# Output projection by token block, and forty first keys of the expert table through dense tiles

## The chip, the cores and the metric

The kernel runs on one core of a Trainium2 chip. The core has five engines that work side by side and wait for one another through semaphores: TensorE (PE in the rows, matrix products into the eight banks of PSUM), VectorE (DVE), ScalarE (ACT), GpSimd (POOL, here used to issue gathers) and SyncE (SP, here used to issue plain transfers). Transfers from HBM run on 16 DMA engines that all queues share. The metric is the device time of one execution in microseconds, lower is better.

## What is computed

One streaming-encoder block over 256 tokens of width 2048, all in float32: a hybrid mixer (stick-breaking attention and HGRN2 recurrence, merged with gates, then `w_out`), a residual with a layer norm, a PEER feed-forward, and another residual with a layer norm. The part that matters here starts at `w_out`:

```python
y = merged @ w_out                                        # 256 x 2048 by 2048 x 2048
x = layer_norm(ALPHA * x + (1 + gate1) * y, ln1_g, ln1_b)
h = x * (1 + scale2) + shift2
q = (h @ w_q).reshape(256, 8, 2, 128)                     # 8 heads, two half keys
s_top, i_top = top_k(einsum('thpd,hpnd->thpn', q, sub_keys), 16)
best, pos = top_k(all 16 x 16 sums of the two halves, 16)
expert_idx = 128 * first_key + second_key                 # 16 experts a head and token
w = softmax(best) * gelu(einsum('td,thkd->thk', h, u_tab[expert_idx]))
y = einsum('thk,thkd->td', w, v_tab[expert_idx])          # tables of 16384 x 2048
x = layer_norm(ALPHA * x + (1 + gate2) * y, ln2_g, ln2_b)
```

## The kernel before

The 256 tokens are two blocks of 128. Up to about 843 us the kernel computes the modulation, the mixer and the gates, which the change leaves alone but for the order of the elements in `merged_t`.

**Output projection.** `w_out` is eight column chunks of 2 MB, streamed by SP through the four slots of `ring` (in `arena`). TensorE multiplies each by both blocks (`project_rows`, L884, 32 products recorded as 64), and between chunks it spreads the modulation rows over the partitions (`spread_mod_rows`, L1039). VectorE adds each chunk to the residual `xr` (L1430, L1433) and, after the last, normalises both blocks. The scale and shift columns for h come from rows that are stored to DRAM (`mod2`) and loaded back.

**First head.** TensorE turns the normed x (`turn`, L1063), makes the query of head 0 (L1079) and its key scores, and VectorE chooses the first 16 experts (`choice`, four pieces). Then POOL gathers. The queries of heads 1 to 7 (`ring`, L1195) follow on TensorE beside that.

**Rows.** There are 16 steps n (block and head) of 16 rows e. A row is one expert of each of 128 tokens. POOL gathers row (n, e) of `expert_u` and row (n-1, e) of `expert_v` (`gather_row`, L535) into two rings of five buffers each. VectorE reduces a u row against h (`reduce_row`, L1561) and ScalarE applies gelu per head. VectorE spreads the 16 weights (`weigh`, L1572). TensorE multiplies the v row into four PSUM banks (`weigh_row`, L1119, 4 products recorded as 8). POOL issues in program order, so a u row that isn't wanted yet holds back the v row behind it. The pieces of the other choices are placed among the rows by `choice_steps`, and a head's u rows wait for its choice (`s_ex`).

**Dense tiles.** Experts whose first key is at or above FIRST_DENSE = 96 are not gathered: `bounds_check` skips those indices. Each of the DENSE = 32 first keys is one tile of 128 experts instead, loaded whole (1 MB) and multiplied by all 256 tokens: first u (`dense_u_piece`, L1141, four pieces a tile, placed by `DENSE_U_AT`), then v (`dense_v_piece`, L1153, placed by `DENSE_V_AT`). 20 of the 32 u tiles stand ahead of step (5, 0) and 12 behind it.

**Mask stage.** In steps n = 5 to 8 the gates of all 256 tokens are spread over the dense tiles: four tokens a row, one product of a column mask and a row mask each (`spread_gates`, L1179). The masks are made by ScalarE and VectorE, with eight column masks in flight, and every BATCH = 16 tokens VectorE multiplies what is in PSUM into the tiles' activations (`weigh_dense`) or, for a tile that comes later, `mix` does. From n = 9 on there are only rows and v tiles, which below is called the v stage. A tail of some 35 us adds, norms and stores.

## Time and profile before

| | us |
|---|---|
| median of 3 runs | 2225.26 |
| lowest, highest | 2222.92, 2225.37 |
| the profiled execution | 2222.43 |
| its span, first to last instruction | 2220.7 |
| mean granted TensorE clock | 0.931 of full speed |
| HBM read over the span | 858.38 MB |

The times of single steps come from the one profiled execution. The profile groups them by engine and line; busy time of TensorE overlaps for neighbouring products, so stretches are read from start to start.

### The profile page before, as it was taken

To read this page: it belongs to the slowest core of one execution; us is meant where nothing else is said; L and a number is where in the kernel's file an instruction comes from. 1 tells how busy PE (TensorE), PEld (TensorE's weight loads), DVE (VectorE), ACT (ScalarE), POOL (GpSimd) and SP (SyncE) were. 2 spreads that over 40 slices of the span, in tenths; PEclk is the share of its full clock that TensorE was granted. 3 is DMA by queue.
4 is the path that set the end of the run, shared out by engine and by line. 5 is a ranking of instruction groups with operands and counts; after the bars stand their busy time and mean duration, and the time that the engine had idled before them with its cause. 6 is when DMAs were issued, how large, how long until landed. Compare 5 with 4: busy or idle time off the path is not lost.

```text
span 2220.7 us, 27840 instructions
## 1 busy us (share of the span) xinstructions
PE 1924.0 (87%) x10667; PEld 1310.0 (59%) x10667; DVE 1353.3 (61%) x2003; ACT 385.3 (17%) x1010; POOL 796.8 (36%) x556
## 2 busy tenths in 40 slices
PE   4899999999999999989788788988975778778776
PEld 4788788888888888878555455555640112112221
DVE  7832377886544541157698898767865544454547
ACT  0122222211000000022132212644430000000001
POOL 1000000000000000014565545776877765656653
PEclk9999999999999999999899999888985888998987
DMA  9973456675765746429899999999999999999997
GB/s 386 423 309 114 155 232 256 264 302 221 284 255 228 278 179 256 160 70 357 329 392 416 409 412 411 405 401 403 386 405 379 405 416 414 402 406 414 400 393 284
DMA packets 104462, 722.47 MB, mean 325 GB/s; under 512 B 29949, under 2 KB 29981, under 8 KB 32045
## 3 DMA queue, kind: packets, MB, share of 16 engines
q0 software_dynamic: 78832, 465.61, 52.7%
q1 hardware_dynamic: 25522, 255.45, 28.8%
q8 instruction: 65, 1.06, 0.2%
q14 instruction: 43, 0.35, 0.0%
HBM read 858.38 MB, written 4.21 MB: 388 GB/s over the span
## 4 chain that ended last, share of the span: by engine, by line
PE 48%; DMA 31%; DVE 8%; issue 7%; POOL 3%; ACT 1%; SPq 0%; POOLq 0%; DVEq 0%
PE ps L876 24%; DMA arena<-expert_v,expert_q 14%; DMA arena<-expert_u,expert 12%; PE ps L884 10%; PE ps L900 4%; PE ps L1119 3%; POOL arena L535 3%; DMA mod_rows<-expert_v,expert_q 2%; DVE work L1561 2%; DMA mod_rows<-expert_u,expert 2%; PE ps L1153 2%; PE ps L1141 1%; PE ps L990 1%; DMA arena<-ada_early 1%; DVE buf_a L1561 1%
## 5 line engine op out<-in xcount | busy, mean ns | idle before, releaser
L1561 DVE CUSTOM_DVE_ANT_0 work<-arena,buf_b 128x2048 f32<-128x2048 f32 x166 | 380.9, 2294 | 266.9 <-DMA arena<-expert_u,expert 266.5
L876 PE MATMUL ps<-buf_a,arena 128*128 128x256 f32 x1920 | 418.5, 379 | 0.9 <-ACT arena L618 0.9
L1119 PE MATMUL ps<-arena,mod_rows 128*32 128x512 f32 x1648 | 254.1, 697 | 188.3 <-DMA arena<-expert_v,expert_q 153.0
L535 POOL DMA_INDIRECT arena<-expert_v,expert_q x206 | 351.7, 1707 | 171.0 <-PE ps L1119 106.9
L876 PEld LDWEIGHTS ps<-buf_a,arena 128*128 128x128 f32 x1920 | 363.5, 190 | 49.9 <-issue 1.2
L535 POOL DMA_INDIRECT arena<-expert_u,expert x205 | 274.7, 1340 | 180.0 <-DVE work L1561 84.4
L523 POOL DMA_DIRECT2D arena<-ada_late x32 | 16.9, 529 | 744.6 <-DVE mod_rows L1313 614.3
L1141 PE MATMUL ps<-arena 128*128 128x256 f32 x1024 | 267.9, 413 | 5.5 <-DMA arena<-dense_u 5.5
L1141 PEld LDWEIGHTS ps<-arena 128*128 128x128 f32 x1024 | 200.0, 203 | 122.2 <-issue 88.6
L1119 PEld LDWEIGHTS ps<-arena,mod_rows 128*32 128x32 f32 x1648 | 38.3, 115 | 300.5 <-DMA arena<-expert_v,expert_q 223.3
L716 ACT ACTIVATE work<-work 32x4 f32<-32x4 f32 (+3 forms) x320 | 66.4, 207 | 556.5 <-DVE work L1561 549.1
L1313 DVE SCALAR_TENSOR_TENSOR mod_rows<-arena,cols,mod_rows 128x4096 f32<-128x4096 f32 x32 | 143.4, 4481 | 13.5 <-DMA arena<-ada_late 10.4
L1153 PE MATMUL ps<-arena 128*32 128x512 f32 x1024 | 133.8, 657 | 0.0
L1561 DVE CUSTOM_DVE_ANT_0 work<-mod_rows,buf_b 128x2048 f32<-128x2048 f32 x42 | 96.4, 2294 | 57.9 <-DMA mod_rows<-expert_u,expert 57.8
L1153 PE MATMUL ps<-arena,buf_a 128*32 128x512 f32 x1024 | 131.2, 646 | 0.0
L884 PE MATMUL ps<-arena,buf_a 128*128 128x256 f32 x512 | 112.3, 379 | 0.0
L876 PE MATMUL ps<-arena 128*128 128x256 f32 x512 | 111.8, 379 | 0.0
L884 PE MATMUL ps<-arena,buf_b 128*128 128x256 f32 x512 | 111.7, 379 | 0.0
L884 PEld LDWEIGHTS ps<-arena,buf_b 128*128 128x128 f32 x512 | 97.1, 190 | 15.7 <-issue 2.8
L900 PE MATMUL ps<-buf_a,arena 128*128 128x256 f32 x384 | 94.7, 411 | 12.3 <-ACT buf_a L591 12.3
L876 PEld LDWEIGHTS ps<-arena 128*128 128x128 f32 x512 | 97.3, 190 | 13.2
L884 PEld LDWEIGHTS ps<-arena,buf_a 128*128 128x128 f32 x512 | 96.9, 190 | 13.0
(256 smaller groups left out, 2078.7 us busy)
## 6 DMA issues: line engine op xcount, KB each, us to landing
arena<-weights SPq DMA_DIRECT2D x62, 2048.0 KB, 8.5
arena<-ada_late POOLq DMA_DIRECT2D x32, 2048.0 KB, 10.4
arena<-ada_early SPq DMA_DIRECT2D x16, 2048.0 KB, 16.9
arena<-dense_u SPq DMA_DIRECT2D x32, 1024.0 KB
arena<-expert_v SPq DMA_DIRECT2D x32, 1024.0 KB
arena<-w_early SPq DMA_DIRECT2D x8, 1536.0 KB, 8.6
arena<-expert_v,expert_q POOLq DMA_INDIRECT x206, 18.3
arena<-expert_u,expert POOLq DMA_INDIRECT x205, 18.3
```

Of the source, the lines that this page charges most:

```text
L523: pool.dma_start(ada_slot[s], ada_late[ds((i * 2 + s) * P, P), g * ADA_COLS:(g + 1) * ADA_COLS])\
L535: pool.indirect_dma_start(slot, None, table, bass.IndirectOffsetOnAxis(ap=indices[:, n // HEADS, column:column + 1], axis=0), bounds_check ...
L716: last = run(target(k, g), source(k, g), function)
L876: last = mm(ps[:, bank, c * TOKENS:(c + 1) * TOKENS], ring[slot][:, first + k, c * P:(c + 1) * P], rhs[:, k, :], start=(k == 0), stop=(k = ...
L884: last = mm(ps[:, bank, b * COLS:(b + 1) * COLS], lhs[:, k, b * P:(b + 1) * P], ring[slot][:, k, :], start=(k == 0), stop=(k == KT - 1))
L900: last = mm(ps[:, c // 2, c % 2 * TOKENS:(c % 2 + 1) * TOKENS], early_slot[g % 2][:, k, c * P:(c + 1) * P], h_t[:, 2 * g + k, :], start=fi ...
L990: last = mm(ps[:, bank + n // 4, n % 4 * P:(n % 4 + 1) * P], decay[:, n, m], decay[:, n, m], start=True, stop=True)
L1119: last = mm(ps[j * GROUP:(j + 1) * GROUP, n // HEADS * QUADS + g, :], spread_w[n % 2][:, e, :], slot[:, j * QCOLS:(j + 1) * QCOLS], start= ...
L1141: last = mm(ps[:, 4 + a % 2, 0:TOKENS], tile[:, k, :], h2_t[:, k, :], start=k == 0, stop=k == KT - 1)
L1153: last = mm(ps[j * GROUP:(j + 1) * GROUP, r, :], dense_act[a // 16][:, a % 16, r * GROUP:(r + 1) * GROUP], dense_slot[t % 2][:, j * QCOLS: ...
L1313: v.scalar_tensor_tensor(out=sums, in0=ada_slot[s], scalar=cond[:, ds(k, 1)], in1=sums, op0=ALU.mult, op1=ALU.add).then_inc(ada_used[s], 1)
L1561: v.tensor_tensor_reduce(out=products[n], in0=u_slot[s], in1=h2[:, n // HEADS], scale=1.0, scalar=0.0, op0=ALU.mult, op1=ALU.add, accum_ou ...
```

## The change

1. The output projection goes by token block (`out_product`, 16 products recorded as 32): all eight chunks for block 0 (`FIRST_OUT`), then the norm of block 0, its turn, the query and the key scores of head 0, and only then the eight chunks for block 1 (`SECOND_OUT`), with the query rows of head 1 of block 0 among them. Chunks 4 and 5 go to the former `ada_slot`s, and chunks 2, 0 and 1 are loaded a second time. VectorE adds the chunks of block 1 between the first 16 u rows (`out_steps`), and the norm of block 1 stands after row (0, 15).
2. U rows use three of their five buffers in the first eight rows (`U_ORDER`), since the others still hold chunks.
3. The scale and shift columns come from 32 one-column products (`mod2_cols`); eight of the twelve spreads and the trip through `mod2` are gone. The residual is stored without the gain and bias of the first norm, and VectorE applies these to the reloaded quarter rows at n = 12 (`residual_gain`, four operations).
4. Choices are made in the order of heads 0, 1 (block 0), 0, 1 (block 1), then 2 to 7 of each (`CHOICE_ORDER`). That of head 2 stands at rows (1, 12) to (1, 15).
5. DENSE is 40, FIRST_DENSE 88. 16 u tiles stand ahead of (5, 0), at (2, 13) to (4, 15), and 24 behind it. BATCH is 8. V tiles start at (9, 4). Reduced rows are written in place.

The core of the diff:

```diff
-DENSE = 32
+DENSE = 40
-BATCH = 512 // DENSE
+BATCH = 8
+FIRST_OUT = ((0, 0, 1), (1, 1, 1), (2, 2, 1), (3, 3, 1), (4, 4, 1), (5, 5, 1), (6, 1, 2), (7, 2, 2))
+SECOND_OUT = ((4, 4, 1), (5, 5, 1), (6, 1, 2), (7, 2, 2), (3, 3, 1), (2, 5, 2), (0, 2, 3), (1, 3, 2))
+UNITS = ((0, 0), (1, 0), (0, 1), (1, 1))
...
+        U_ORDER = [(0, 1, U_RING - 1)[row % 3] if row < TOPK // 2 else (row - 1) % U_RING for row in range(BLOCKS * HEADS * TOPK + TOPK)]
...
-        choice_steps = row_order[4:12:2] + [row_order[TOPK + i * 64 // 56] for i in range(56)]
-        dense_steps = [row_order[TOPK + FIRST_BESIDE + 1:5 * TOPK], row_order[5 * TOPK:9 * TOPK - 4]]
+        CHOICE_ORDER = [0, 1, HEADS, HEADS + 1] + list(range(2, HEADS)) + list(range(HEADS + 2, BLOCKS * HEADS))
+        choice_steps = row_order[12:16] + row_order[TOPK + 4:TOPK + 60]
+        out_steps = {(0, 0): 9, (0, 2): 10, (0, 4): 11, (0, 7): 12, (0, 11): 13, (0, 14): 14, (0, 15): 15}
+        dense_steps = [row_order[2 * TOPK + SECOND_BESIDE + 1:5 * TOPK], row_order[5 * TOPK:9 * TOPK - 4]]
-        v_steps = row_order[10 * TOPK - 3:16 * TOPK - 3]
+        v_steps = row_order[9 * TOPK + QUADS:16 * TOPK - 3]
-        BEFORE_MASKS = 20
+        BEFORE_MASKS = 16
-        ACT_DELAY, MIX_DELAY = 2, 6
+        ACT_DELAY, MIX_DELAY, STEPS_OF_BATCH = 2, 3, 2
...
+            def out_product(j):
+
+                b, (c, s, fill) = j // GATES, (FIRST_OUT + SECOND_OUT)[j]
+                if s >= 4:
+                    pe.wait_ge(late_out_loaded[s - 4], fill * 16)
+                else:
+                    pe.wait_ge(loaded[s], (F_OUT[s] + fill) * 16)
+                if j > 3:
+                    pe.wait_ge(s_y, j - 2)
+                if GATES <= j < GATES + TURNED:
+                    pe.wait_ge(s_h2, j - GATES + 1)
+                for k in range(KT):
+                    last = mm(ps[:, j % 4, 0:COLS], merged_t[:, b, k, :], ring[s][:, k, :], start=k == 0, stop=k == KT - 1)
+                last.then_inc(s_om, 1)
...
+            for j in range(GATES):
+                out_product(j)
+            spread_gate2()
+            mod2_cols(range(KT, 2 * KT)).then_inc(s_mcol, 1)
...
             turn(0, range(TURNED))
-            pe.wait_ge(loaded[0], (F_QUERY[0] + 1) * 16)
-            pe.wait_ge(s_row, 1 + 13)
-            query_of_first(0)
-            turn(1, (0, 1))
+            pe.wait_ge(s_row, 1 + 5)
+            query_rows(0)
+            turn_back(0, (0, 1))
             turn_query(0)
-            turn(1, (2, 3))
+            turn_back(0, (2, 3))
             pe.wait_ge(s_sk, 16)
...
+            score_first(0)
+            for j in range(GATES, GATES + 5):
+                out_product(j)
+            query_rows(1)
             turn_query(1)
...
+            out_product(GATES + 5)
+            score_first(1)
+            out_product(GATES + 6)
+            out_product(GATES + 7)
```

On TensorE, from the spread of the modulation rows to the first query. L1039 is a spread, L884 a chunk with both blocks, L1063 a turn, L1079 the query of head 0. Before:

```order
L1039 MATMUL ps<-mod_rows,cst 128x512 x4
L884 MATMUL ps<-arena,buf_b 128x256 x32
L1039 MATMUL ps<-mod_rows,cst 128x512 x3
L884 MATMUL ps<-arena,buf_b 128x256 x32
L1039 MATMUL ps<-mod_rows,cst 128x512 x2
...
L884 MATMUL ps<-arena,buf_b 128x256 x96
L1063 MATMUL ps<-cst,buf_a 128x128 x16
L1079 MATMUL ps<-arena 128x256 x16
L1063 MATMUL ps<-cst,buf_a 128x128 x8
```

The same place after (L1094 is a spread, L1105 the one-column products, L1120 `out_product`, L1099 the spread of gate2, L1138 a turn, L1157 query rows, L1145 a turn back, L1165 and L1175 the turn and scores of a query):

```order
L1094 MATMUL ps<-mod_rows,cst 128x512 x4
L1105 MATMUL ps<-cols,mod_rows 128x1 x16
L1120 MATMUL ps<-arena,buf_b 128x256 x128
L1099 MATMUL ps<-mod_rows,cst 32x512 x4
L1105 MATMUL ps<-cols,mod_rows 128x1 x16
L1138 MATMUL ps<-cst,buf_a 128x128 x16
L1157 MATMUL ps<-arena 128x256 x16
...
L1175 MATMUL ps<-work 128x128 x2
L1120 MATMUL ps<-arena,buf_b 128x256 x80
L1157 MATMUL ps<-arena 128x256 x16
```

Before the first turn stand 128 products of the projection instead of 256; 80 of the rest stand behind the scores of head 0, in one piece.

On TensorE in the mask stage, before (L1119 the v row, L1141 pieces of a u tile, L1179 the tokens' gates):

```order
L1119 MATMUL ps<-mod_rows 32x512 x4
L1179 MATMUL ps<-mod_rows 128x32 x4
L1119 MATMUL ps<-arena,mod_rows 32x512 x4
L1141 MATMUL ps<-arena 128x256 x4
L1179 MATMUL ps<-mod_rows 128x32 x4
L1119 MATMUL ps<-arena,mod_rows 32x512 x4
L1141 MATMUL ps<-arena 128x256 x4
L1179 MATMUL ps<-mod_rows 128x32 x4
```

After (L1210, L1242 and L1280 are the same three):

```order
L1210 MATMUL ps<-mod_rows 32x512 x4
L1242 MATMUL ps<-arena 128x256 x4
L1280 MATMUL ps<-mod_rows 128x40 x4
L1210 MATMUL ps<-arena,mod_rows 32x512 x4
L1242 MATMUL ps<-arena 128x256 x8
L1280 MATMUL ps<-mod_rows 128x40 x4
L1210 MATMUL ps<-arena,mod_rows 32x512 x4
L1242 MATMUL ps<-arena 128x256 x4
```

Every row now has one or two pieces of a tile (96 in 60 rows), where it had none or one (48).

On VectorE, in the first 16 rows after the change (L1645 is a reduced row, L1529 and L1531 add a chunk of block 1, L1536 its statistics):

```order
L1620 CAST expert<-work 128x16
L1529 SCALAR_TENSOR_TENSOR work<-mod_rows,ps 128x256
L1531 SCALAR_TENSOR_TENSOR buf_a<-buf_a,work 128x256
L1645 ISA arena,work<-arena,buf_b 128x2048
L1645 ISA work 128x1
L1529 SCALAR_TENSOR_TENSOR work<-mod_rows,ps 128x256
L1531 SCALAR_TENSOR_TENSOR buf_a<-buf_a,work 128x256
L1536 BN_STATS small<-buf_a 128x6
L1645 ISA arena,work<-arena,buf_b 128x2048
```

Before, nothing of the projection was left at this place.

## Rows read from the trace of the kernel before

**Rows 1.** The page: busy time by engine, and its 40 slices of the span.
```profile
PE 1924.0 (87%) x10667; PEld 1310.0 (59%) x10667; DVE 1353.3 (61%) x2003; ACT 385.3 (17%) x1010; POOL 796.8 (36%) x556
...
PE   4899999999999999989788788988975778778776
...
DMA  9973456675765746429899999999999999999997
```

**Rows 2.** Windows of the three stages: start:end and length, busy us, granted clock, DMA share, GB/s.
```profile
1388.70:1672.00 283.30, 240.12 (x1414) 159.75 (x1414) 205.82 (x335) 133.79 (x387) 209.33 (x129) 0.88 1.00 400
...
995.70:1388.70 393.00, 332.52 (x1669) 225.29 (x1667) 328.55 (x778) 90.86 (x261) 218.85 (x154) 0.96 0.97 389
1672.00:2190.00 518.00, 390.20 (x2992) 96.07 (x2992) 268.87 (x251) 24.22 (x113) 337.67 (x227) 0.85 1.00 400
```

**Rows 3.** Timeline of TensorE, output projection to first query: start, us, operation, records, idle before.
```profile
847.02 13.98 PE L884 MATMUL ps<-arena,buf_b 128*128 128x256 f32 x64
...
924.51 41.71 PE L884 MATMUL ps<-arena,buf_b 128*128 128x256 f32 x192
971.44 3.68 PE L1063 MATMUL ps<-cst,buf_a 128*128 128x128 f32 x16 [5.23 <-DVE buf_a L1452]
```

**Rows 4.** One-column products: duration min/median/max of the line before that has them.
```profile
L893 PEld LDWEIGHTS ps<-cols,work x64: 186/192/337, 24.2 to 126.6; 128*128 128x128 f32 x64
```

**Rows 5.** Timeline of POOL: the first gather.
```profile
995.65 2.17 POOL L535 DMA_INDIRECT arena<-expert_u,expert  x1 [12.95 <-DVE expert L1534]
```

**Rows 6.** Timeline of VectorE: first u row, last of head 0, first of head 1.
```profile
1004.14 2.29 DVE L1561 CUSTOM_DVE_ANT_0 buf_b<-arena,buf_b 128x2048 f32<-128x2048 f32 x1 [4.94 <-DMA arena<-expert_u,expert]
...
1056.57 2.29 DVE L1561 CUSTOM_DVE_ANT_0 buf_b<-arena,buf_b 128x2048 f32<-128x2048 f32 x1
...
1073.30 2.29 DVE L1561 CUSTOM_DVE_ANT_0 buf_a<-arena,buf_b 128x2048 f32<-128x2048 f32 x1 [14.44 <-DMA arena<-expert_u,expert]
```

**Rows 7.** The page: the software queue's bytes, and a gather's us from issue to landing.
```profile
q0 software_dynamic: 78832, 465.61, 52.7%
...
arena<-expert_u,expert POOLq DMA_INDIRECT x205, 18.3
```

**Rows 8.** Timeline of TensorE in the mask stage: two rows of the loop, back to back.
```profile
1406.09 1.07 PE L1119 MATMUL ps<-arena,mod_rows 128*32 128x512 f32 x8
1407.09 1.99 PE L1141 MATMUL ps<-arena 128*128 128x256 f32 x8
1408.92 0.97 PE L1179 MATMUL ps<-mod_rows 128*128 128x32 f32 x8
1409.82 1.06 PE L1119 MATMUL ps<-arena,mod_rows 128*32 128x512 f32 x8
```

**Rows 9.** Waits of TensorE in 1388:1672: in total, times, longest.
```profile
PE ps L1119 <- DMA arena<-expert_v,expert_q: 33.0, 17, 8.5
PE ps L1119 <- DVE mod_rows L1572: 5.2, 2, 3.3
PE ps L1165 <- DVE mod_rows L1572: 2.5, 1, 2.5
```

**Rows 10.** Timeline of TensorE after a long wait, at the end of the mask stage.
```profile
1660.00 1.93 PE L1119 MATMUL ps<-arena,mod_rows 128*32 128x512 f32 x8 [8.46 <-DMA arena<-expert_v,expert_q]
```

**Rows 11.** L1141 alone, in the mask stage: busy us of its products and weight loads.
```profile
1388.70:1672.00 283.30, 110.29 (x384) 78.62 (x384) 0.88 1.00 400
```

**Rows 12.** Timeline of TensorE in the v stage: a quarter of a v tile.
```profile
1750.09 1.89 PE L1153 MATMUL ps<-arena 128*32 128x512 f32 x16
```

More of the change, by code:

```diff
@@ new lines, in first_keep, with query_head @@
+            def first_keep(u, signal):
+                act_e.wait_ge(s_ks0, u + 1)
+                keep(*UNITS[u], slice(0, 2)).then_inc(signal, 1)
+            def query_head(h):
+                s = h % 2
+                act_e.wait_ge(used[s], 1 + F_QUERY[s] + h // 2 + 1)
+                run(pq_t[s], ps[:, 6 + s, :], ACT.Copy).then_inc(s_pq, 1)
+                act_e.wait_ge(s_ks, h - 1)
+                for b in range(BLOCKS):
+                    last = keep(h, b, slice(0, 2))
+                last.then_inc(s_kept, 1)
@@ L1122, in weigh_row @@
                 last.then_inc(slot_used, 1)
+            pe.wait_ge(s_wgt, 1)
+            pe.wait_ge(s_h2, TURNED + 1)
+            for e in range(2):
+                weigh_row(0, e)
+            query_rows(3)
+            turn_query(3)
+            for e in range(2, QUADS):
+                weigh_row(0, e)
+            score_first(3)
             def turn_stats(turn, groups):
@@ L1188, in score_half @@
                 return last
[L1190 removed]
+            for h in range(2, HEADS):
                 s = h % 2
[L1192 removed]
+                pe.wait_ge(loaded[s], (F_OUT[s] + 2 + s + h // 2) * 16)
                 for i in range(4):
@@ L1222, in _ @@
                     pe.wait_ge(s_dw, BATCHES)
-                for e in range(FIRST_BESIDE if n == 1 else 0, TOPK):
+                for e in range(SECOND_BESIDE if n == 2 else 0, TOPK):
                     weigh_row(n - 1, e)
```

457 lines of the change are left out of this document (243 added, 214 removed).

## Prediction

> **What bounds the kernel now.** I read the page first, then windows of the stages, then timelines where two engines meet. The page's slices [rows 1] show two halves: TensorE at 9 tenths and a half-busy DMA up to about 970 us, then a DMA at 9 tenths to the end with TensorE at 7 to 9. The windows [rows 2] make that exact: 389 GB/s from the first gather to the mask stage, 400 GB/s in the mask stage and 400 GB/s in the v stage, with a DMA share of 0.97 to 1.00. From 996 us on the time is bytes divided by 0.4 MB/us. What the kernel can gain is (a) fewer bytes, (b) an earlier first gather. What can take it back is TensorE: in the mask stage it is busy 240.1 of 283.3 us, and the change puts more work there. So the sum is three terms: when the mask stage starts, how long it lasts, how long the v stage lasts. The tail doesn't change.
>
> **Bytes.** The software queue moved 465.6 MB [rows 7]. Less the 32 late modulation loads of 2 MB (67.1) and some 3 MB of other things that leaves 395.5 of the 536.9 MB that 512 full rows of 1.049 MB would be, so 0.736 is gathered. The reference's own choice on its inputs gives 0.736 as well for first keys below 96, and 0.675 below 88. Each row loses 0.061 x 1.049 = 0.064 MB. All 512 rows lose 33 MB, 8 more u tiles and 8 more v tiles add 16.8, and three reloaded chunks of `w_out` add 6.3. The net is only -10 MB, or 25 us.
>
> **Term 1, start of the mask stage (1388.7 before).** The projection runs from 847.0 and its last three chunks start at 924.5 and take 41.7 us [rows 3], so it ends at 966.2 and a chunk of both blocks is 13.8 us, a block's share 6.9. After the change the first part is 16 one-column products, eight chunk halves and nothing else. A one-column product is two records, and a weight load is 192 ns [rows 4], so 32 records are 6.1 us, then 8 x 6.9 = 55.3: it ends at 908.6. From the projection's end to the first gather at 995.65 [rows 5] the chain is 29.4 us (norm 5.2, turn, query, scores, choice), and it stays, but the turn now stands behind the gate2 spread (1.1) and 6.1 us of one-column products, where the norm covers 5.2: +2. The store of the residual, which is new ahead of the kept scores, has some 10 us of turn and query to land and costs nothing; without that cover it would be about 7 us. **First gather 940.0, 55.7 us earlier.**
>
> From there to the mask stage were 393 us. (1) Bytes: 154 rows lose 9.9 MB, four u tiles fewer 4.2, three chunks more +6.3: -7.8 MB at 389 GB/s is -20 us. The chunk loads run beside u rows when the DMA isn't full. (2) With three buffers, a round of three rows is a landing of 8.5 us (issue 995.65 to reduction 1004.14, [rows 5, 6]) plus 2.3 for the reduction and some 2 for the issue: 13 us, 4.3 a row, where 16 rows took 1058.8 - 1004.1 = 55 us or 3.4 a row. The ninth row also waits for the sixth chunk of block 1. I take +12, between 0 (the DMA was the limit anyway) and +20. (3) The norm of block 1 now waits for the last row of head 0, and VectorE can't start head 1 before the turn of block 1. It idled 14.4 us there already, for a gather [rows 6]; I take +0. (4) The u rows of head 2 wait for a choice that ends with row (1, 15), with all buffers empty and POOL's v rows behind them. What is queued behind POOL's wait is both streams. A gather lands in 18.3 us under load [rows 7], less on an empty DMA; about a third of it is covered by rows in flight: +12, from 0 to +22. ScalarE's queue holds the key scores of heads 3 to 7 behind softmaxes of that order, so TensorE goes at VectorE's pace here; it has 48 v rows and 16 tiles to do afterwards and isn't late. TensorE's own work in the stretch, 332.5 us before, changes by +55 (block 1) and -30 (four tiles at 7.4): 358 of 397, which fits. **Mask stage at 940 + 393 - 20 + 24 = 1337, -52.** Ends: -76 (no loss) and -20 (both losses at their upper end, and TensorE late by a further 14).
>
> **Term 2, the mask stage (283.3 us).** At full clock TensorE needs 1.0 us for a v row, 1.83 for a piece of a u tile and 0.90 for four tokens' gates, 3.73 in all [rows 8]. Before: 64 x 1.9 + 48 x 1.83 = 209; it was busy 240 (clock 0.88, [rows 2]) and idle 43, of which 33 waiting for v rows [rows 9]. After: 64 x 1.9 + 96 x 1.83 = 297. The DMA needs 128 rows x 0.708 + 24 tiles x 1.049 = 115.8 MB, 289 us. TensorE becomes the longer of the two, by a little. To its 297 I add the waits at the heads' ends that no transfer makes (5.2 + 2.5 [rows 9] and 2 for ScalarE's copies, 9.7) and half of the 31 us that the slow clock cost. After an idle of 8.46 us a v row takes 1.93 instead of 1.07 [rows 10, 8], which is 1.2 against 2.4 GHz, and with the long waits gone fewer such stretches should be left. **322 us, +39.** Ends: 289, +6 (everything behind the DMA) and 283 + 110 = 393, +110, where 12 tiles at the 9.2 us that each took here (110.3 for 12, [rows 11]) come on top in full. I take the middle because the rows at 1406 to 1409 show TensorE without a gap at exactly this place. VectorE, 205.8 busy, gets some 15 us of smaller batches and more mixes, beside 77 us of idle time: nothing, unless its order against TensorE binds (rival C).
>
> The Trainium skill (Perfetto Trace Analysis, Identifying the Most-Contended Engine) holds that TensorE's matmul busy time is no measure of its headroom and that the busy share of weight loads is. By that the mask stage has headroom: weight loads are busy 159.8 of 283.3 us, and 12 more tiles would bring about 239.
>
> **Term 3, the v stage (518 us).** Some 230 of its rows lose 14.8 MB, 8 v tiles add 8.4: -6.4 MB at 400 GB/s, **-16 us**. TensorE gets 8 x 4 quarters at 1.9 [rows 12] = 61 us, which makes 451 of 502. That is hidden by the 128 us in which it was idle, but nine tenths full; without that cover it is +45. The four gain operations of 2.3 us on VectorE (268.9 busy of 518) are hidden. Four such operations leave the front, behind which nobody waited.
>
> **Sum.** The profiled execution took 2222.4 (1.7 above its span), the median is 2225.3. 2222.4 - 52 + 39 - 16 = 2193.4. Runs scatter 1 to 3 us above that: 2194.
>
> **Rivals.** **A, forecast:** the mask stage turns TensorE-bound and eats three quarters of the early start. 0.50, 2194, with 2170 to 2218 for itself. **B, TensorE stays hidden:** the mask stage follows the bytes, 2222 - 52 + 6 - 16 = 2156. For it: DMA share 1.00 and 33 us of TensorE's idle time are waits for transfers. Against: 297 us of work don't fit in 289. The rule cited above would give this case. 0.17. **C, slower, lockstep:** in the mask stage VectorE can't make masks more than eight tokens (two rows) ahead of TensorE, and a batch is now two rows, so TensorE's first token of batch i+2 waits for a product that VectorE makes one row earlier, where it had two rows' slack. VectorE's own rows wait for u gathers, and each wait passes to TensorE, whose clock falls again. Then the tiles come on top in full: 2222 - 52 + 110 - 16 = 2264. It decides from a mask stage of 351 us on (283 + 68). Against it: before, VectorE's masks made TensorE wait nowhere in this stage; the only VectorE entries of rows 9 are the heads' ends. 0.13. **D, the front keeps little:** three buffers, the late norm and the late choice cost 56 us instead of 24, the mask stage starts at 1369 and the sum is 2222 - 20 + 39 - 16 = 2225, no change. 0.15. **E, the bytes don't fall,** because skipped indices cost time though no bytes: 25 us lost and the tiles' 17 MB paid, 2194 + 83 = 2277. Against: gathers of 0.736 rows ran at the same 400 GB/s as everything else. 0.05.
>
> **How the numbers follow.** A measurement can tell about 0.2% (4.5 us) from no change. Faster by more holds all of A and B but its edge and a third of D: 0.72; within 0.2%: 0.10; slower: C, E and what D has above 2230: 0.18. The range takes in B's centre and D's: 2150 to 2232, with the tails of B, C and E left out.
>
> **What would show it.** First gather near 940; mask stage from about 1337 with TensorE near 93% busy, a clock above 0.90, a DMA share around 0.9 instead of 1.00 and hardly a wait for v rows; a v stage near 500 us at 400 GB/s. A DMA share of 1.00 in a mask stage of 290 us says B. Waits of L1280 for masks or of TensorE for `weigh_dense` say C. A hole in the DMA before row (2, 0) much longer than 15 us says D.

## The result, and the profile after

| | before | after |
|---|---|---|
| median, 10 runs each | 2224.86 us | 2233.05 us |
| lowest, highest | 2221.40, 2226.86 | 2228.72, 2238.11 |
| the profiled execution | 2222.43 | 2238.11 |
| its span | 2220.7 | 2236.4 |
| mean granted clock | 0.931 | 0.954 |

The change makes the kernel slower by 0.4%: the ratio is 1.0042, with a 95% interval of 1.0030 to 1.0054. 2194 was forecast, with 2150 to 2232 as the range. The direction was wrong, and the time lies just above the range.

The profiled execution of after is the slowest of its ten, 5 us above the median; that of before lies 2 us below its own. Times of stages come from one execution each, here and for every kernel below, so a few us in them are noise. What a kernel is worth is told by the medians and ratios.

The page after has these lines, beside [rows 1] and [rows 7]:

```profile
PE 1978.3 (88%) x11486; PEld 1368.9 (61%) x11486; DVE 1369.4 (61%) x2117; ACT 381.4 (17%) x1050; POOL 772.0 (35%) x555
...
DMA  9973366675765747288587999999999999999997
...
q0 software_dynamic: 78688, 430.58, 49.3%
...
HBM read 879.86 MB, written 4.19 MB: 395 GB/s over the span
```

The row of DMA shows where to look. Before, the pause ahead of the first gather is the 2 in slice 18 of 40, and 9, 8 and nines follow. After, the 2 stands in slice 17, and behind it come 8, 8, 5, 8, 7 before the nines begin in slice 23. The windows of the three stages make it exact (columns as in [rows 2]):

```profile
939.30:1386.20 446.90, 360.60 (x1807) 254.01 (x1806) 334.77 (x804) 93.49 (x297) 211.41 (x155) 0.90 0.85 331
1386.20:1690.90 304.70, 297.46 (x1799) 219.14 (x1797) 222.69 (x444) 137.86 (x411) 181.45 (x125) 0.99 0.98 381
1690.90:2207.60 516.70, 412.87 (x3504) 108.61 (x3504) 278.36 (x255) 24.23 (x113) 350.28 (x233) 0.94 1.00 397
```

From here on every kernel is told by the same marks of its profiled execution: the start of the first gather, the first product of the mask stage, the first product behind that stage, and the end of the span.

| us | first gather | front | mask stage | rest | span |
|---|---|---|---|---|---|
| before | 995.7 | 393.0 | 284.6 | 547.4 | 2220.7 |
| after, as forecast | 940 | 397 | 323 | 531 | 2192 |
| after | 939.3 | 446.9 | 304.7 | 545.5 | 2236.4 |

Against the forecast the front lost 50, the mask stage gave back 19 and the rest lost 14: 2193.4 + 50 - 19 + 14 = 2238, which is the profiled execution. Of the 56.4 us by which the first gather comes earlier, 446.9 - 393.0 = 53.9 are gone when the mask stage starts. "Front" is the stretch from the first gather to the mask stage.

**Where the front went.** The waits in the front of after, in all, times and the longest, show engines that wait for one another (first the waiting engine, its operand and line, then whom it waits for):

```profile
ACT mod_rows L741 <- DVE mod_rows L1606: 186.0, 15, 23.1
POOL arena L570 <- PE ps L1210: 93.7, 25, 20.5
DVE arena L1645 <- DMA arena<-expert_u,expert: 72.7, 22, 7.2
...
PE ps L1287 <- ACT work L856: 47.4, 4, 15.7
...
POOL arena L570 <- DVE expert L1620: 30.0, 2, 16.9
...
PE ps L1138 <- ACT buf_a L879: 26.7, 1, 26.7
```

In the front of before the same wait of TensorE, for the copy of a query, was small:

```profile
PE ps L1186 <- ACT work L822: 9.8, 4, 7.8
```

Read them as a ring. L741 is the exponential of a head's softmax on ScalarE; it waits for the end of that head's choice on VectorE (L1606). L856 is ScalarE's copy of a query, which TensorE needs (L1287) to turn and score it. L1210 is a v row on TensorE, whose end frees the buffer that POOL gathers into. The timelines show the links. On ScalarE, with the idle time before in brackets:

```profile
1078.39 0.22 ACT L741 ACTIVATE mod_rows<-mod_rows 128x16 f32<-128x16 f32 x1 [14.35 <-DVE mod_rows L1606]
1078.51 0.58 ACT L856 ACTIVATE work<-ps 128x512 f32<-128x512 f32 x1
...
1104.98 0.22 ACT L741 ACTIVATE mod_rows<-mod_rows 128x16 f32<-128x16 f32 x1 [23.07 <-DVE mod_rows L1606]
1105.10 0.58 ACT L856 ACTIVATE work<-ps 128x512 f32<-128x512 f32 x1
...
1141.42 0.22 ACT L741 ACTIVATE mod_rows<-mod_rows 128x16 f32<-128x16 f32 x1 [21.82 <-DVE mod_rows L1606]
1141.54 0.58 ACT L856 ACTIVATE work<-ps 128x512 f32<-128x512 f32 x1
```

Each query's copy starts 0.12 us after the start of the softmax that it stands behind, and its products had been ready for long: TensorE had been idle for 15.7, 5.6 and 15.1 us by then. On TensorE, the first and the last of the three:

```profile
1079.14 2.08 PE L1287 MATMUL ps<-work 128*128 128x128 f32 x8 [15.72 <-ACT work L856]
...
1142.17 2.07 PE L1287 MATMUL ps<-work 128*128 128x128 f32 x8 [15.06 <-ACT work L856]
```

On POOL, the issue of gathers:

```profile
939.29 1.08 POOL L570 DMA_INDIRECT arena<-expert_u,expert  x1 [21.77 <-issue]
...
1017.77 0.99 POOL L570 DMA_INDIRECT arena<-expert_u,expert  x1 [13.08 <-DVE expert L1620]
...
1087.10 0.99 POOL L570 DMA_INDIRECT arena<-expert_v,expert_q  x1 [20.53 <-PE ps L1210]
...
1117.33 0.99 POOL L570 DMA_INDIRECT arena<-expert_u,expert  x1 [16.89 <-DVE expert L1620]
...
1151.03 0.99 POOL L570 DMA_INDIRECT arena<-expert_v,expert_q  x1 [17.56 <-PE ps L1210]
```

TensorE stands still for 15 us on a copy, so no v buffer comes free, so POOL stands still at a v row for 20.5 and 17.6 us with the next u rows behind it. Then VectorE gets no u rows, and since the pieces of a choice stand among u rows on VectorE, the choice is late, the softmax is late, and the next copy is late. The two entries of 13.1 and 16.9 us are holes of the other kind, POOL at the first u row of heads 1 and 2 before its choice was done. The wait of 26.7 us is TensorE's for the normed block 1; in before it had waited 5.2 us for both blocks [rows 3].

### The profile page after: what moved, and what is told of

The parts are those of the page before. It is cut to its first block, busy times and chain, and to the rows that moved or that the text cites. A ratio compares the mean times of both kernels' runs of the same rounds, so it can differ in the third digit from the quotient of the medians.

```text
span 2236.4 us, 29519 instructions
## 1 busy us (share of the span) xinstructions
PE 1978.3 (88%) x11486; PEld 1368.9 (61%) x11486; DVE 1369.4 (61%) x2117; ACT 381.4 (17%) x1050; POOL 772.0 (35%) x555
## 3 DMA queue, kind: packets, MB, share of 16 engines
q0 software_dynamic: 78688, 430.58, 49.3%
## 4 chain that ended last, share of the span: by engine, by line
PE 62%; DMA 24%; DVE 6%; issue 4%; POOL 2%; ACT 1%; SPq 0%; POOLq 0%; DVEq 0%
PE ps L937 24%; DMA arena<-expert_v,expert_q 10%; PE ps L1242 10%; DMA arena<-expert_u,expert 8%; PE ps L1210 5%; PE ps L945 5%; PE ps L1120 4%; PE ps L961 4%; DMA mod_rows<-expert_u,expert 3%; PE ps L1296 2%; POOL arena L570 2%; DVE arena L1645 2%; DMA mod_rows<-expert_v,expert_q 2%; PE ps L1280 2%; PE ps L1157 1%
## 5 line engine op out<-in xcount | busy, mean ns | idle before, releaser
L1645 DVE CUSTOM_DVE_ANT_0 arena<-arena,buf_b 128x2048 f32<-128x2048 f32 x204 | 467.1, 2292 | 300.2 <-DMA arena<-expert_u,expert 299.2
L570 POOL DMA_INDIRECT arena<-expert_v,expert_q x206 | 333.6, 1619 | 230.8 <-PE ps L1210 164.3
L570 POOL DMA_INDIRECT arena<-expert_u,expert x204 | 262.4, 1286 | 202.6 <-DVE work L1645 80.6
L1210 PE MATMUL ps<-arena,mod_rows 128*32 128x512 f32 x1648 | 229.9, 635 | 92.7 <-DMA arena<-expert_v,expert_q 74.5
L1242 PE MATMUL ps<-arena 128*128 128x256 f32 x1280 | 306.0, 390 | 4.8 <-DMA arena<-dense_u 4.8
L1242 PEld LDWEIGHTS ps<-arena 128*128 128x128 f32 x1280 | 237.8, 192 | 116.1 <-issue 79.8
L562 POOL DMA_DIRECT2D arena<-ada_late x32 | 16.9, 529 | 747.0 <-DVE mod_rows L1410 615.8
L1645 DVE CUSTOM_DVE_ANT_0 mod_rows<-mod_rows,buf_b 128x2048 f32<-128x2048 f32 x52 | 119.2, 2293 | 74.2 <-DMA mod_rows<-expert_u,expert 73.9
L755 ACT ACTIVATE work<-work 32x4 f32<-32x4 f32 (+2 forms) x336 | 69.5, 207 | 527.9 <-DVE work L1645 492.9
L1210 PEld LDWEIGHTS ps<-arena,mod_rows 128*32 128x32 f32 x1648 | 37.1, 111 | 195.7 <-DMA arena<-expert_v,expert_q 133.5
L1254 PE MATMUL ps<-arena,buf_a 128*32 128x512 f32 x1024 | 121.8, 610 | 0.0
L1254 PE MATMUL ps<-arena 128*32 128x512 f32 x1024 | 121.8, 610 | 0.0
L1120 PE MATMUL ps<-arena,buf_b 128*128 128x256 f32 x512 | 112.9, 383 | 0.0
L937 PE MATMUL ps<-arena 128*128 128x256 f32 x512 | 111.8, 379 | 0.0
L1120 PEld LDWEIGHTS ps<-arena,buf_b 128*128 128x128 f32 x512 | 98.2, 192 | 13.5
L937 PEld LDWEIGHTS ps<-arena 128*128 128x128 f32 x512 | 97.3, 190 | 13.2
```

What stands on the lines that cost most here:

```text
L570: pool.indirect_dma_start(slot, None, table, bass.IndirectOffsetOnAxis(ap=indices[:, n // HEADS, column:column + 1], axis=0), bounds_check ...
L755: last = run(target(k, g), source(k, g), function)
L937: last = mm(ps[:, bank, c * TOKENS:(c + 1) * TOKENS], ring[slot][:, first + k, c * P:(c + 1) * P], rhs[:, k, :], start=(k == 0), stop=(k = ...
L1120: last = mm(ps[:, j % 4, 0:COLS], merged_t[:, b, k, :], ring[s][:, k, :], start=k == 0, stop=k == KT - 1)
L1210: last = mm(ps[j * GROUP:(j + 1) * GROUP, n // HEADS * QUADS + g, :], spread_w[n % 2][:, e, :], slot[:, j * QCOLS:(j + 1) * QCOLS], start= ...
L1242: last = mm(ps[:, 4 + a % 2, 0:TOKENS], tile[:, k, :], h2_t[:, k, :], start=k == 0, stop=k == KT - 1)
```

## The experiments

Ten kernels were run. The first four share 17 runs of before (median 2225.96 us), the second four share 11 (2222.61), the last two 7 (2222.07). Each edit is shown against the kernel named with it; longer ones are shown in part, with dots where lines are left out.

### ScalarE's order alone

Against after: each softmax goes behind the copy and the key scores of the next query, and gelu(1) and the first gates go one head later with it.

```diff
             for h in range(2, HEADS):
                 query_head(h)
-                if h == 3:
+                if h == 4:
                     gelu(1)
+                if h > 2:
+                    soft_exp(h - 1)
                 if h == 5:
                     experts_to_quads(2)
-                if h < HEADS - 1:
-                    soft_exp(h)
-                if h == 5:
+                if h == 6:
                     gates_to_quads(2)
```

> The changed kernel with one difference, on ScalarE: the softmax exponential of head h stands behind the key scores of head h+1 instead of ahead of them, and gelu(1) and the first gates to quads one head later. Theory S (ScalarE's queue paces TensorE in the query heads, which starves the gathers): TensorE's waits for the query copy, 47 us between 940 and 1386, fall below 15, the mask stage starts at about 1355 instead of 1386 and the time is about 2205. Rival H (the gathers are held by the order of the choices and the three buffers, and ScalarE's queue only fills a wait that is there anyway): the mask stage starts at 1378 or later and the time stays within 8 us of 2233.

Measured: 2213.38 us (2210.78 to 2219.25), ratio to before 0.9949 [0.9935, 0.9964]. That is 20 us less than after, by the order of a few small instructions on an engine that is busy 17% of the time. The theory had 2205 and the rival a time within 8 us of 2233, so the truth lies between them and nearer the theory. The front is 430.0 us instead of 446.9, the mask stage 304.4. Its waits in the front, for the two entries of the ring:

```profile
ACT mod_rows L741 <- DVE mod_rows L1606: 108.8, 14, 14.9
...
PE ps L1287 <- ACT work L856: 18.7, 2, 15.3
```

47.4 us of TensorE waiting for the copies became 18.7. The ring is a cause, and it isn't all of it: 430 is still 33 more than the 397 of the forecast. One long wait of 15.3 us is left; it belongs to head 2, whose query stands behind the softmax of head 1 of block 1. POOL's waits for v buffers and for the choices hardly fell (93.7 to 85.4 us, and 30.0 to 30.3).

### The order alone and the tiles alone

The first is after with 32 first keys through tiles, 16 of them ahead of the mask stage, the second is before with 40, 16 of them ahead of the mask stage (with the smaller batches and the rows in place that 40 tiles need).

```diff
-DENSE = 40
+DENSE = 32
```

> The changed kernel with DENSE = 32: the new order of the projection and the first heads, 16 u tiles ahead of the mask stage and 16 in it, gathers below first key 96. If the order is what lost the time, as the trace of the changed kernel says (mask stage at 1386 where 1337 was forecast), it starts its mask stage as late or later (about 1395, 10 MB more gathered), spends 290 us there by bytes, and ends at about 2240. If the tiles are what lost it, it is at or below 2225.

```diff
-DENSE = 32
+DENSE = 40
-BATCH = 512 // DENSE
+BATCH = 8
...
-        BEFORE_MASKS = 20
+        BEFORE_MASKS = 16
...
-        ACT_DELAY, MIX_DELAY = 2, 6
+        ACT_DELAY, MIX_DELAY, STEPS_OF_BATCH = 2, 3, 2
...
-                v.tensor_tensor_reduce(out=products[n], in0=u_slot[s], in1=h2[:, n // HEADS], scale=1.0, scalar=0.0,
+                v.tensor_tensor_reduce(out=u_slot[s], in0=u_slot[s], in1=h2[:, n // HEADS], scale=1.0, scalar=0.0,
```

> The kernel before with 40 dense first keys, 16 u tiles ahead of the mask stage and 24 in it, batches of 8 tokens, rows reduced in place; order of the projection and the first heads as before. Theory (tiles gain by bytes, the order loses): the mask stage starts about 36 us earlier than 1389 (14 MB less at 389 GB/s), lasts about 305 as in the changed kernel, and the v stage gains up to 16: about 2200. Rival (the tiles gain nothing, since what the DMA gives TensorE takes): 2222 or above.

Measured: the order alone 2239.72 us, ratio 1.0071 [1.0056, 1.0086]; the tiles alone 2226.59 us, ratio 1.0008 [0.9998, 1.0018].

| us | first gather | front | mask stage | rest | span |
|---|---|---|---|---|---|
| order alone | 936.6 | 456.7 | 296.8 | 547.9 | 2238.0 |
| tiles alone | 998.3 | 372.0 | 304.1 | 547.4 | 2221.8 |

So the loss is the order's, and it is in the front. The tiles are worth nothing: what they take from the front (21 us, fewer tiles and fewer bytes there) they put into the mask stage (19.5 us), and the rest doesn't change. 2200 was expected of them, and the rival's 2222 or more came. The mask stage of the tiles alone takes the same 304.1 as that of after, 304.7, whatever stood ahead of it:

```profile
998.30:1370.30 372.00, 311.83 (x1540) 204.73 (x1538) 328.35 (x778) 89.39 (x257) 237.61 (x154) 0.93 0.96 378
1370.30:1674.40 304.10, 298.20 (x1798) 219.72 (x1798) 225.03 (x444) 137.70 (x411) 205.53 (x126) 0.98 0.97 376
1674.40:2190.00 515.60, 410.89 (x3484) 108.42 (x3488) 266.44 (x245) 24.23 (x113) 332.63 (x229) 0.92 0.99 394
```

### What a skipped row costs

Before, with every index above 0 skipped: 395 MB of gathered rows aren't moved, and the result holds nothing of the gathered experts.

```diff
-                                        bounds_check=GATHERED - 1, oob_is_err=False)\
+                                        bounds_check=0, oob_is_err=False)\
```

> The kernel before with every gathered index but 0 skipped, so that the rows' products are of stale data: what is left out is the transfer of the rows. It shows what the rows' time is without their bytes. If a skipped index costs no more than its share of issue, DMA busy falls to the dense tiles and the weights, and the stretch from the first gather to the end is bound by TensorE and VectorE: about 1000 us instead of 1225. If skipped indices cost transfer time (rival E of the prediction), the gathers keep landing 10 us or more after issue under a busy DMA. The HBM read count tells as well whether skipped rows are read: 858 MB less 395 if not, about 858 if so.

Measured, in one execution: 2114.44 us, with 364.4 in the front, 270.6 in the mask stage and 481.6 in the rest. Without 395 MB the kernel is only 111 us faster, where 0.4 MB/us would make it nearly 1000; the expectation, with 225 us, had twice the gain. The queue's line on its page, and the window of its v stage:

```profile
q0 software_dynamic: 78832, 70.58, 10.1%
...
HBM read 858.38 MB, written 4.21 MB: 408 GB/s over the span
```

```profile
1631.00:2080.00 449.00, 363.33 (x2992) 95.24 (x2992) 269.91 (x252) 24.24 (x113) 379.83 (x228) 0.89 0.23 71
```

The DMA engines are busy 0.23 of the time there and the stage still takes 449 us. Without the bytes another engine sets the pace, and POOL's timeline shows which:

```profile
1803.27 0.99 POOL L535 DMA_INDIRECT arena<-expert_u,expert  x1 [0.30 <-issue]
1804.57 2.15 POOL L535 DMA_INDIRECT mod_rows<-expert_v,expert_q  x1 [0.30 <-issue]
1807.03 2.03 POOL L535 DMA_INDIRECT arena<-expert_u,expert  x1 [0.30 <-issue]
1809.36 0.99 POOL L535 DMA_INDIRECT arena<-expert_v,expert_q  x1 [0.30 <-issue]
1810.66 2.80 POOL L535 DMA_INDIRECT arena<-expert_u,expert  x1 [0.30 <-issue]
```

POOL issues one gather behind the other with 0.30 us between and is busy 379.8 of 449 us; 228 gaps of 0.30 are another 68. 449 us are thus all POOL. The v stage of before took 518 us for as many gathers, 15% more. But POOL is not that near its limit there: it was busy only 337.67 us [rows 2], which with the same gaps is 406 of 518, and for some 130 us it waited for buffers. A gather of skipped rows alone took POOL longer (1.67 us in the mean of this stage against 1.49 in before), so 449 us is no floor of before.

The packets of the queue are as many as before (78832), so a skipped row is still a packet. The records of the single packets in the two traces say of what kind. In before the queue has 48244 packets of 8192 bytes, in the mean of 324 ns each, and 26092 of 4 bytes, in the mean of 9 ns; here it has none of 8192 bytes, and 48244 more of 4 bytes. So a skipped row is a packet of 4 bytes, and on the DMA engines it takes 3% of the time of a full one. The 48244 are 0.736 of the 65536 rows of 128 tokens and 512 gathers, as the prediction had it. The HBM reads are the same 858.38 MB, though 395 MB fewer arrived.

### The bytes alone

Before with its 32 tiles, and gathers that skip first keys from 88 on; the experts with first keys 88 to 95 are left out of the result. It is the change's saving of 33 MB without the tiles that pay for it.

```diff
-                                        bounds_check=GATHERED - 1, oob_is_err=False)\
+                                        bounds_check=88 * N_KEYS - 1, oob_is_err=False)\
```

> The kernel before with gathers skipped from first key 88 on instead of 96, and still 32 dense tiles, so that the experts of eight first keys are left out of the result. It isolates 33 MB fewer gathered bytes without any more work for TensorE. If the rows go by bytes at 0.4 MB/us, as the prediction had it: -82 us, about 2143, of which -24 us lie ahead of the mask stage, -20 in it and -37 in the v stage. If POOL's issue and TensorE are nearly as long as the DMA (all rows skipped saved only 108 us, not the 990 of the bytes): about half of it or less, 2180 or above, with the v stage no more than 18 us shorter.

Measured: 2182.71 us (2175.50 to 2185.57), ratio 0.9814 [0.9796, 0.9832], 40 us less than before, where 33 MB at 0.4 MB/us are 82. By stages: front 378.1 (15 less, forecast bytes 9.9 MB or 25 us), mask stage 276.5 (8 less), rest 524.8 (22.6 less, forecast bytes 14.8 MB or 37 us). So a byte saved by skipping was worth about half of a byte moved (0.5 by the medians, 0.4 in the mask stage, 0.6 in the other two). The queue's line and the v stage:

```profile
q0 software_dynamic: 78832, 432.67, 50.8%
...
HBM read 858.38 MB, written 4.21 MB: 397 GB/s over the span
```

```profile
1650.60:2143.00 492.40, 374.21 (x2968) 94.21 (x2972) 266.38 (x245) 24.23 (x113) 350.72 (x226) 0.88 0.99 391
```

The DMA is full (0.99) and moves 391 GB/s, where before moved 400. The page's queue line gives the same as a price: before 52.7% of 2220.7 us for 465.61 MB, 2.51 us of all engines a MB; here 50.8% of 2175.4 us for 432.67 MB, 2.55; after 49.3% of 2236.4 us for 430.58 MB, 2.56. The packets' records agree: 4022 of them went from 8192 to 4 bytes, and the mean of the full ones rose from 323.5 to 329.0 ns, while their median stayed at 309. So it is a minority of them that takes longer. The eight traces of kernels that gather below first key 88 have means of 328.4 to 330.4 ns, the three of kernels that gather below 96 (before, the order alone, the repaired order with 32) 323.5 to 324.1. The 4022 packets would have been 81 us of all engines at the old mean; the slower ones among the rest and the small packets take 17 back.

### The norm earlier, then the choice earlier

Two steps on top of ScalarE's order. First, head 1's choice starts at row (0, 8) instead of (0, 12), and the last chunks of block 1 and its norm come at row (0, 12) instead of (0, 15).

```diff
-        choice_steps = row_order[12:16] + row_order[TOPK + 4:TOPK + 60]
-        out_steps = {(0, 0): 9, (0, 2): 10, (0, 4): 11, (0, 7): 12, (0, 11): 13, (0, 14): 14, (0, 15): 15}
+        choice_steps = row_order[8:12] + row_order[TOPK + 4:TOPK + 60]
+        out_steps = {(0, 0): 9, (0, 2): 10, (0, 4): 11, (0, 7): 12, (0, 9): 13, (0, 11): 14, (0, 12): 15}
...
-                    if (n, e) == (0, TOPK - 1):
+                    if (n, e) == (0, 12):
                         mean_and_variance(1)
```

> The kernel of the run with ScalarE's order changed (2213), and also the choice of head 1 at rows (0, 8) to (0, 11) and the last sums and the norm of block 1 at row (0, 12) instead of behind (0, 15). Theory: the 31 us that TensorE waits for the normed block 1 shrink to below 20, POOL no longer waits 14 us for the choice of head 1, and the front is 10 to 12 us shorter: about 2202. If the front goes by bytes, the time stays at 2213.

Second, the choices of block 1's first heads take two pieces a row, so that all later ones, head 2's first, come four rows earlier; and the query of head 2 goes ahead of the softmax that was left in its way.

```diff
-        choice_steps = row_order[8:12] + row_order[TOPK + 4:TOPK + 60]
+        choice_steps = row_order[8:12] + [row_order[TOPK + 4 + i // 2] for i in range(8)] + row_order[TOPK + 8:TOPK + 56]
...
+            query_head(2)
             soft_exp(HEADS + 1)
             for h in range(2, HEADS):
-                query_head(h)
+                if h > 2:
+                    query_head(h)
...
-                    if (n, e) in choice_steps:
+                    for _ in range(choice_steps.count((n, e))):
                         next(picks, None)
```

> The same, and the choices of block 1's heads 0 and 1 at two pieces a row, so that the choice of head 2 ends with row (1, 11) instead of (1, 15), with ScalarE's key scores of head 2 ahead of the softmax of block 1's head 1. Theory: the wait of POOL for the choice of head 2 (16 us) and TensorE's wait for the query of head 2 (15 us) go, another 12 to 15 us, about 2190. If only one hole can be seen at a time (the DMA was filling up behind it), under 5 us.

Measured: the first 2208.82 us, ratio 0.9935 [0.9921, 0.9949], front 424.3; with the second 2192.63 us (2190.01 to 2195.02), ratio 0.9866 [0.9849, 0.9884], front 400.4, mask stage 304.7, rest 548.3. The norm and head 1's choice were a small thing (3 us by the ratios, 5 by the medians). The late choice of head 2 with the last stuck query was a large one (16 us). Since they were changed together, how much each of the two made isn't settled. 2202 was expected of the first, for which TensorE's wait for the normed block 1 was to fall below 20 us; it fell from 31.0 to 24.1. 2190 was expected of the second, and both waits that it was aimed at went: POOL's for the choice of head 2 from 16.5 to 5.2 us, and TensorE's of 16.0 us for the query of head 2 altogether.

Two windows of the front side by side, first of after, then of this kernel:

```profile
1000.00:1100.00 100.00, 65.43 (x340) 47.38 (x340) 73.27 (x179) 27.50 (x95) 37.06 (x30) 0.81 0.75 281
1100.00:1200.00 100.00, 68.34 (x337) 48.38 (x334) 68.75 (x184) 18.17 (x66) 35.40 (x28) 0.83 0.73 283
```

```profile
1000.00:1100.00 100.00, 87.83 (x468) 62.82 (x468) 91.02 (x225) 31.06 (x101) 58.43 (x41) 0.93 0.97 379
1100.00:1200.00 100.00, 87.03 (x444) 56.77 (x445) 91.61 (x242) 25.39 (x87) 50.59 (x40) 0.95 0.95 365
```

TensorE, VectorE and the DMA all do about a third more in the same 200 us. In after none of them was at its limit. What the whole kernel computes is the same; only its order differs.

### Tiles in other shares, and the repaired order without them

Three kernels against the last one: 20 tiles on either side of the mask stage's start instead of 16 and 24, 18 and 22, and 32 tiles instead of 40.

```diff
-        BEFORE_MASKS = 16
+        BEFORE_MASKS = 20
```

> The same again with 20 u tiles on each side of the start of the mask stage instead of 16 and 24. The mask stage, in which TensorE waits for no transfer, loses 4 tiles at 7.4 us (about -20 until the DMA binds at 290), the stretch ahead of it gets 4 tiles of 1.05 MB under a full DMA (+10) and TensorE there becomes tight: about 2182. If TensorE already binds ahead of the mask stage, the sum is zero.

```diff
-        BEFORE_MASKS = 16
+        BEFORE_MASKS = 18
```

> The kernel of the run with all choices early, with 18 u tiles ahead of the mask stage and 22 in it (16 and 24 gave 2193, 20 and 20 gave 2190). In the trace of 16 and 24 TensorE is the longer in the mask stage (304.7 us against 289 by bytes); in that of 20 and 20 the mask stage is 290 by bytes, and the front is 21 us longer for 4 tiles, twice their bytes. 18 and 22 should meet both ends: mask stage about 297, front about 408, 2187. If the sum is flat, 2190 to 2193.

```diff
-DENSE = 40
+DENSE = 32
```

> The kernel of the run with all choices early (2193), with DENSE = 32: 16 u tiles ahead of the mask stage and 16 in it. With the order as it was, the 8 tiles gained nothing on the kernel before (2227 against 2226) and 7 us on the changed order (2240 to 2233). If that holds with the front repaired, this runs at about 2200: 10 MB more gathered ahead of the mask stage (+15 to +25), a mask stage of 297 instead of 305, a v stage as long. If the tiles pay only where the front is full of transfers, it is at 2210 or above.

| | time, us | ratio to before | front | mask stage | rest |
|---|---|---|---|---|---|
| 16 and 24 | 2192.63 | 0.9866 [0.9849, 0.9884] | 400.4 | 304.7 | 548.3 |
| 18 and 22 | 2189.52 | 0.9848 [0.9822, 0.9875] | 406.5 | 299.6 | 545.8 |
| 20 and 20 | 2189.79 | 0.9846 [0.9831, 0.9862] | 421.3 | 290.3 | 542.1 |
| 16 and 16 | 2192.35 | 0.9862 [0.9837, 0.9886] | 405.6 | 300.5 | 547.3 |

Moving a tile only moves its time: the intervals overlap, and no share can be called better. Gathering eight first keys instead of having tiles for them changes nothing either, as in before. The expectations were 2182 for 20 tiles, 2187 for 18 and 2200 for the kernel with 32, so the tiles were thought to be worth more than they are. In the unrepaired order they are worth 6.7 us (2239.72 to 2233.05). The windows of 20 and 20:

```profile
935.30:1356.50 421.20, 380.77 (x1935) 271.82 (x1934) 335.33 (x804) 93.32 (x299) 212.87 (x155) 0.96 0.95 366
1356.50:1646.90 290.40, 270.96 (x1675) 195.16 (x1675) 221.01 (x441) 136.79 (x404) 214.45 (x128) 0.98 0.98 382
```

TensorE's waits for v rows in the mask stage, 1.4 us in all with 24 tiles, are here

```profile
PE ps L1212 <- DMA arena<-expert_v,expert_q: 13.3, 5, 8.7
```

With four tiles fewer TensorE is no longer what the mask stage waits for: it is busy 271 of 290 us and waits for transfers. The DMA share alone wouldn't tell, for it is 0.98 with 24 tiles as well. The versions with 18 and 20 tiles ahead have the lowest medians, 33 us (1.5%) below before, and both kernels of the case are beaten by all four.

## Why the prediction was wrong

**The first gather was right.** 940.0 was forecast, 939.3 came. The pieces, on TensorE:

```profile
849.39 3.63 PE L1105 MATMUL ps<-cols,mod_rows 128*128 128x1 f32 x32
852.88 57.19 PE L1120 MATMUL ps<-arena,buf_b 128*128 128x256 f32 x256
```

Eight chunk halves took 57.2 us against 55.3 worked out. 32 records of one-column products took 3.6 instead of 6.1: the price was taken from weight loads of 192 ns [rows 4], and here the records follow one another every 0.11 us. The part began at 849.4 and not at 847.0, and the chain behind it took 29.2 us instead of 31.4. That these small misses cancel to 0.7 us is luck; the other kernels with this order have their first gather at 935.3 to 938.9.

**Term 1, the start of the mask stage, is the step that failed.** Forecast 1337, measured 1386.2. The failed part is the sum of its losses: +24 in the forecast, and by the same subtraction, 446.9 - (393 - 20), 74 in the run (this execution was 5 us above the median, and some of that may be in it). The sentence that broke is the one in (4) that TensorE goes at VectorE's pace here and isn't late. The text had seen that ScalarE's queue holds the key scores behind softmaxes, but it costed that at nothing, because TensorE's work in the stretch (358 of 397 us) fitted. Busy time can't answer this; the question is which engine waits for which. In before ScalarE copied query 3 ahead of the softmax of head 1, and query 5 ahead of that of head 2. After the change the copy of every query from head 2 on stands behind the softmax of an earlier choice, and such a softmax waited up to 23 us. Putting ScalarE's order right gave 17 us of the front, the norm and head 1's choice 6, the choice of head 2 with its query 24: together 47 of the 50. By the medians of the whole kernel the three were worth 20, 5 and 16 us, so the split is good to some 5 us. With all three the front takes 400.4. That this is near the forecast's 397 doesn't confirm its sum, since the late choice, for which it took +12, is no longer in that kernel.

**(2), the three buffers, came as forecast.** The 16 rows of head 0, first reduction to the end of the last:

```profile
944.98 2.29 DVE L1645 CUSTOM_DVE_ANT_0 arena<-arena,buf_b 128x2048 f32<-128x2048 f32 x1 [5.96 <-DMA arena<-expert_u,expert]
...
1010.76 2.29 DVE L1645 CUSTOM_DVE_ANT_0 mod_rows<-mod_rows,buf_b 128x2048 f32<-128x2048 f32 x1
...
1025.08 2.29 DVE L1645 CUSTOM_DVE_ANT_0 arena<-arena,buf_b 128x2048 f32<-128x2048 f32 x1 [2.50 <-DMA arena<-expert_u,expert]
```

They took 68.1 us where 55 had been read in before: +13 for a forecast of +12. The gap ahead of head 1 is 12.0 us on VectorE, where it was 14.4, as (3) had it with its +0. So only some 8 us of the 54 are lost by the first row of head 1 (85.8 us from the first gather, against 77.7), and the rest behind it.

**(4) had the hole in the right place.** The choice of head 2 holds POOL for 16.9 us, and the one of head 1, which the forecast didn't name, for 13.1. It took +12 for the first. What it missed, as the timelines read, is that a hole isn't paid once: the rows that come late make the next choice late. No run shows the choice of head 2 by itself.

**The bytes of Term 1** were priced at 20 us for 7.8 MB. The tiles alone, which save 14.1 MB in the front (9.9 of rows, 4.2 of tiles), got 21 us there, where 389 GB/s gives 36. At that rate 21 us are saved, and the three reloaded chunks, 6.3 MB, cost 16 at 389 GB/s, so 5 are left of the 20. That would put some 15 of the 50 us here and not to the waits; it is an estimate, and no run parts the two.

**Term 2, the mask stage, had the mechanism right and the size wrong.** Forecast +39, measured +20. TensorE needs 64 x 1.9 + 96 x 1.83 = 297 us, and the window says 297.46 busy in 304.70. What was too much are the allowances on top: 10 us for the heads' ends and 15 for the slow clock. The waits of TensorE in this stage of after are

```profile
PE ps L1210 <- DMA arena<-expert_v,expert_q: 1.3, 2, 0.7
PE ps L1266 <- ACT cst L811: 1.0, 1, 1.0
PE ps L1210 <- ACT cst L811: 1.0, 1, 1.0
```

and the granted clock is 0.99, where it was 0.88. With the waits went nearly all of the clock's loss and not half. The DMA share stayed at 0.98, not 0.9: DMA and TensorE end this stage almost together.

**Rival B** is refuted in its mechanism, though its price was nearer than the forecast's (+6 against +39, where +20 was measured; its sum, by the way, is 2160 and not 2156). With 24 tiles TensorE waits 1.3 us for transfers, with 20 it waits 13.3. But the two are close: four tiles are 16 pieces or 29 us of TensorE's time, and without them the stage was 14 shorter, of which their bytes alone are about 11. The Trainium skill's rule that was cited for it (Perfetto Trace Analysis, Identifying the Most-Contended Engine: judge TensorE's headroom by the busy share of its weight loads, beside the share of peak arithmetic, and not by that of its products) doesn't hold in this trace as far as the weight loads go. Weight loads are busy 219.14 of 304.70 us, 72%, while the products leave 7 us. In these float32 products of 256 columns a load of 0.19 us lies under a product of 0.23 (1.83 us for eight), so that share stays well under 100% in this mix though the engine has hardly a gap.

**Rival C**, the lockstep in the mask stage, doesn't happen: nothing in the waits above is for VectorE's masks. It named a ring of engines, but in the wrong stage. **Rival D** had the right stage. Its sign, a hole in the DMA ahead of row (2, 0) much longer than 15 us, wasn't there: POOL stood still for 16.9 us, but the DMA was nearly empty for only about 10 us (a share of 0.80 from 1105 to 1110 us, 0.04 and 0.20 in the next two stretches of 5 us, 0.91 behind them). D took 56 us for the losses of the front, where 74 came. Its causes are the buffers, the norm and the choice, and ScalarE's order, worth 20 us by the medians, isn't among them.

**Term 3, the v stage, is mis-sized.** Forecast -16, measured -2. The 14.8 MB of skipped rows were worth 22.6 us by the bytes alone, not 37. Eight v tiles of 1.049 MB would cost 21 us at 400 GB/s, and 22.6 - 21 is nearly nothing, as measured; the v tiles weren't tried by themselves. **Rival E** said that skipped indices cost time; it was right that they save less than their bytes, and far too dear. The 0.736 of the rows that before moves at 400 GB/s didn't speak against it, since that only shows that the DMA engines are busy, not what the same time would have moved with no row skipped.

What isn't settled is why a saved byte is worth only about half. Two readings can be weighed with the traces. A small packet costs next to nothing by itself (9 ns), so that isn't it. POOL's issue isn't it either: in the v stage of the bytes alone POOL was busy 350.7 of 492 us and waited 89 us for buffers. What is seen is that a minority of the full packets take longer. HBM reads that happen for skipped rows all the same would fit that, and the counter says 858.38 MB for before, for 33 MB less and for 395 MB less. But with all rows skipped, the 228 gathers of the v stage would then be 239 MB of reads in 449 us, with the tiles some 600 GB/s, and no slice of any page has more than 430. That speaks for a counter of what is asked for and not of what is read. The cause stays open.

## What to carry to other kernels

When a reordering moves one stage's results later, go through every engine that waits for them and ask what is queued behind that wait; here an engine at 17% held up one at 81% and one at 75% of the front, and the sum of busy times said nothing of it. When the waits form a ring through the buffers, look at the next steps too before a hole gets a price. In this kernel a row that a gather skips was worth about half its bytes, and the tiles that replaced such rows won 0 to 7 us, so measure the skipped rows by themselves before they are traded for full transfers. Where the DMA and an engine are both nearly full, ask the engine's waits which of them sets the time: the DMA share was 0.98 with TensorE waiting 1 us for transfers, and with 13.

## What the runs showed of the hardware

A gather with skipped indices still issues a packet a row (78832 in the queue with 465.61, 432.67 or 70.58 MB moved). That of a skipped row has 4 bytes and took 9 ns in the mean, where one of 8192 bytes took 324. The page's HBM reads don't fall with them (858.38 MB in all three). Issuing a gather of 128 rows took POOL 1.0 to 2.8 us in the lines shown, with 0.30 us between; with all rows skipped, POOL's issue alone filled a v stage of 449 us. TensorE's granted clock was 0.99 in a stage in which it had 7 us of 305 free, and 0.81 and 0.83 in stretches of the front in which it stood still for 15 us at a time. One-column products of float32 with weights of 128 x 128 followed one another every 0.11 us.
